# Values as the stationary operand in column tiles, and a gate that is turned instead of the heads, in the banded attention stage of a three-block kernel

## The reference, cut to what matters

```python
def swa_with_sinks(q, k, v, sinks):        # W = 128 queries a block, 256 keys for each
    ...
    s = jnp.where(mask[None, :, None, None], s, -jnp.inf)
    m = jnp.maximum(jnp.max(s, axis=-1, keepdims=True), sink)
    p = jnp.exp(s - m)
    denom = jnp.sum(p, axis=-1, keepdims=True) + jnp.exp(sink - m)
    p = (p / denom).astype(v.dtype)
    o = jnp.einsum('bnhgqk,bnkhd->bnqhgd', p, vw)
    return o.reshape(B, T, Hq * D)

# in first_block
o_a = swa_with_sinks(q_a, k_a, v_a, sinks[layer]) * jax.nn.silu(ag)
mix = jnp.concatenate([o_h, o_a], axis=-1)
out = jnp.einsum('bte,ed->btd', mix, w_out[layer])
```

## Time and profile before

| what | value |
|---|---|
| median of 3 runs | 4453.24 us (4452.0 to 4453.49) |
| the profiled execution, its own time | 4439.21 us |
| its span, first to last instruction | 4437.4 us |
| TensorE busy | 4089.6 us (92%), 26938 instructions |
| TensorE weight load busy | 3431.6 us (77%) |
| VectorE busy | 2470.0 us (56%) |
| ScalarE busy | 1464.4 us (33%) |
| GpSimd busy | 503.9 us (11%) |
| mean granted TensorE clock | 0.968 of 2.4 GHz |
| stage of the change in the trace | about 545 us to 1170 us of the span |

### The profile page before, as it was taken

How to read it: one execution, slowest core, us unless ns; L and a number is a source line. 1 busy time by engine, 2 the same in 40 slices (tenths; PEclk the granted TensorE clock), 3 DMA queues, 4 the chain that set the end, 5 groups by cost and what they waited for, 6 DMA issues and landing times. The chain is left out here.

```text
span 4437.4 us, 71865 instructions
## 1 busy us (share of the span) xinstructions
PE 4089.6 (92%) x26938; PEld 3431.6 (77%) x26938; DVE 2470.0 (56%) x5058; ACT 1464.4 (33%) x3233; POOL 503.9 (11%) x509
## 2 busy tenths in 40 slices
PE   9999889999699996999989978999898998999989
PEld 7888678888577775999878867778786776777767
DVE  5444444444467665777643347778643443677733
ACT  4232322222222222455521126666522221322221
POOL 0000011111100000122211100000000101122200
PEclk9999999999899998999989989999999999999989
DMA  4111321111434333121322244100045223323233
GB/s 151 50 66 50 109 94 64 64 64 64 150 126 145 121 127 102 50 69 57 123 97 111 112 141 144 39 20 29 17 169 183 102 104 138 127 90 102 90 136 118
DMA packets 218618, 434.72 MB, mean 98 GB/s; under 512 B 36803, under 2 KB 90692, under 8 KB 218278
## 3 DMA queue, kind: packets, MB, share of 16 engines
q1 hardware_dynamic: 218406, 431.89, 28.4%
HBM read 248.20 MB, written 146.93 MB: 89 GB/s over the span
## 5 line engine op out<-in xcount | busy, mean ns | idle before, releaser
L265 PE MATMUL rp_pj<-rp_w_high,rp_hT_high 128*128 128x512 f32 (+1 forms) x640 | 236.6, 379 | 23.2 <-DVE rp_gate L1443 17.8
L2652 DVE TENSOR_SCALAR_CACHE_REDUCE fa_sm<-fa_sc 128x512 f32<-128x512 f32 (+2 forms) x320 | 194.6, 610 | 92.7 <-PE fa_sc L2493 81.8
L265 PE MATMUL fp_pj<-fp_w_high,fp_hT_high 128*128 128x512 f32 (+2 forms) x640 | 216.6, 353 | 23.4 <-DMA fp_hT_low<-kept_low_dram 20.0
L266 PE MATMUL rp_pj<-rp_w_low,rp_hT_high 128*128 128x512 f32 (+1 forms) x640 | 231.7, 371 | 0.0
L266 PE MATMUL fp_pj<-fp_ahead_w_low,fp_hT_high 128*128 128x512 f32 (+2 forms) x640 | 214.7, 350 | 0.0
L265 PE MATMUL hg_pj<-hg_w_high,hg_hT_high 128*128 128x512 f32 x512 | 208.3, 407 | 5.2 <-DVE hg_w_low L255 5.2
L2600 ACT CAST fa_pT_high<-fa_tp 128x512 fp32r<-128x512 f32 (+1 forms) x288 | 160.9, 559 | 149.6 <-PE fa_tp L2507 147.5
L2507 PE MATMUL fa_tp<-fa_ident,fa_sm 128*128 128x128 f32 x1088 | 176.1, 283 | 31.9 <-DVE fa_pT_low L201 15.6
L265 PE MATMUL rc_pj<-rc_w_high,rc_hT_high 128*128 128x512 f32 (+1 forms) x512 | 190.6, 380 | 15.0 <-DMA rc_ident<-const_ident 10.0
L266 PE MATMUL hg_pj<-hg_w_low,hg_hT_high 128*128 128x512 f32 x512 | 201.5, 394 | 0.0
L2507 PEld LDWEIGHTS fa_tp<-fa_ident,fa_sm 128*128 128x128 f32 x1088 | 125.1, 142 | 93.4 <-DVE fa_pT_low L201 40.9
(11 more groups left out here) (590 smaller groups left out, 10843.8 us busy)
## 6 DMA issues: line engine op xcount, KB each, us to landing
rw_given<-rw_packed_dram SPq DMA_DIRECT2D x48, 512.0 KB, 3.7
rc_back<-rc_XB SPq DMA_DIRECT2D x48, 336.0 KB
rw_packed_dram<-rp_M SPq DMA_DIRECT2D x48, 256.0 KB, 2.6
rp_M<-rp_U SPq DMA_DIRECT2D x16, 728.0 KB, 4.7
hg_xt<-in_x SPq DMA_DIRECT2D x16, 512.0 KB, 3.6
kept_x_high_dram<-hg_hT_high SPq DMA_DIRECT2D x16, 512.0 KB, 3.5
kept_x_low_dram<-hg_hT_low SPq DMA_DIRECT2D x16, 512.0 KB, 4.3
sw_hT_high<-kept_x_high_dram SPq DMA_DIRECT2D x16, 512.0 KB, 3.6
```

The costliest lines, as they stand in the source:

```text
L265: pe.matmul(out, hT.high[:, kc, :], high[:, kc, lo:hi], start=kc == 0, stop=False)
L266: pe.matmul(out, hT.high[:, kc, :], low[:, kc, lo:hi], start=False, stop=False)
L2652: dve.tensor_scalar(sm[:, to:to + cols], bank_of(slot)[:, 0:cols], 0.0, NEG, ALU.add, ALU.max, accum_out=tops[:, four, c:c + 1]).then_inc( ...
```

## The change

The stationary and the moving operand of `weigh` change places. The values (128 keys x 64 numbers) become stationary, and the turned probabilities of two heads (128 keys x 256 columns) move. The 64 output numbers go to partitions 0 to 63 for even heads and to 64 to 127 for odd ones, so two neighbouring matmuls lie in different column tiles of the array. There are 8 matmuls instead of 16, and `ov` comes out with the head's numbers on its partitions and the queries in its columns.

So the result needs no turning, but the gate does, and the reciprocal sums, which are one number for each query and head, have to be multiplied into something that still has the queries on its partitions. VectorE multiplies the gate by `rden` into `gated` (between the reciprocal and its first copy of probabilities). TensorE turns `gated` into the bank `th` (`turn_gate`, between `turn_p` of rounds 2 and 3 and block 1 of `project_out`). ScalarE copies it to `gatedT` (between its copies of probabilities and the tanh). After `weigh`, one VectorE instruction makes `mixaT` from `ov` and `gatedT`, ScalarE rounds `mixaT` to `mixT.high`, and `low_of_mix` subtracts that from `mixaT`, both in SBUF. `turn_a` and the two instructions on `mixa` are gone. The semaphores follow; `turn_qk` now waits for the copies of the tile before, and `turn_hg` for `gatedT_ready`, since `th` is used twice in a tile.

```diff
--- before.py
+++ after.py
@@ -703,7 +703,9 @@
         sm = sb("sm", [P, SW_HEADS, 2 * P])
         top, negtop, sinkd, expsink, total, rden = (sb(n, [P, SW_HEADS]) for n in ("top", "negtop", "sinkd", "expsink", "total", "rden"))
         pT = sb("pT", [P, 2 * SW_HEADS, P])
-        mixa = sb("mixa", [P, SW])
+        gated = sb("gated", [P, SW])
+        gatedT = sb("gatedT", [P, 4, P])
+        mixaT = sb("mixaT", [P, 4, P])
         mixT = Parts(s, "mixT", [P, KC, P], STATIONARY)
         z = sb("z", [P, D])
         stats = sb("stats", [P, 2, 6])
@@ -725,7 +727,8 @@
         roped, v_kept, qk_turned, qT_ready, kT_ready = sem("roped"), sem("v_kept"), sem("qk_turned"), sem("qT_ready"), sem("kT_ready")
         scored, masked, top_ready, p_ready, den_ready = sem("scored"), sem("masked"), sem("top_ready"), sem("p_ready"), sem("den_ready")
         p_turned, pT_act, pT_dve, weighed, mixa_ready = sem("p_turned"), sem("pT_act"), sem("pT_dve"), sem("weighed"), sem("mixa_ready")
-        hg_turned, hgT_ready, a_turned, aT_ready = sem("hg_turned"), sem("hgT_ready"), sem("a_turned"), sem("aT_ready")
+        gated_ready, gate_turned, gatedT_ready = sem("gated_ready"), sem("gate_turned"), sem("gatedT_ready")
+        hg_turned, hgT_ready, aT_ready = sem("hg_turned"), sem("hgT_ready"), sem("aT_ready")
         out_done, z_ready, var_ready, rstd_ready, y_ready = sem("out_done"), sem("z_ready"), sem("var_ready"), sem("rstd_ready"), sem("y_ready")
         y_scaled = sem("y_scaled")
 
@@ -800,14 +803,15 @@
 
             def turn_qk(t, pt):
                 pe.wait_ge(roped, t + 1)
-                need(pe, aT_ready, t)
+                need(pe, pT_dve, 2 * t)
+                need(pe, pT_act, 2 * t)
                 for j in range(4):
                     pe.transpose(tp[0][:, j * P:(j + 1) * P], qkv[:, j * P:(j + 1) * P], ident[:])
                 pe.transpose(tp[1][:, 0:P], qkv[:, SW:SW + SW_KV], ident[:]).then_inc(qk_turned, 1)
 
             def turn_hg(t):
                 pe.wait_ge(hg_here, 16 * (t + 1))
-                need(pe, hgT_ready, t)
+                need(pe, gatedT_ready, t)
                 for c in range(4):
                     last = pe.transpose(th[:, c * P:(c + 1) * P], hgm[:, c * P:(c + 1) * P], ident[:])
                 last.then_inc(hg_turned, 1)
@@ -853,24 +857,26 @@
                         last = pe.transpose(tp[n % 2][:, m * P:(m + 1) * P], sm[:, k // 2, (k % 2) * P:(k % 2 + 1) * P], ident[:])
                     last.then_inc(p_turned, 1)
 
+            def turn_gate(t):
+                pe.wait_ge(gated_ready, t + 1)
+                pe.wait_ge(hgT_ready, t + 1)
+                for c in range(4):
+                    last = pe.transpose(th[:, c * P:(c + 1) * P], gated[:, c * P:(c + 1) * P], ident[:])
+                last.then_inc(gate_turned, 1)
+
             def weigh(t):
                 pe.wait_ge(pT_act, 2 * t + 2)
                 pe.wait_ge(pT_dve, 2 * t + 2)
                 pe.wait_ge(v_kept, t + 1)
                 need(pe, mixa_ready, t)
-                for j in range(4):
-                    for g in range(2):
-                        h = 4 * g + j
-                        for slot in range(2):
-                            last = pe.matmul(ov[:, h * SW_DIM:(h + 1) * SW_DIM], pT[:, 2 * (2 * j + g) + slot, :],
-                                             vr[:, slot, g * SW_DIM:(g + 1) * SW_DIM], start=slot == 0, stop=slot == 1)
+                for g in range(2):
+                    for slot in range(2):
+                        for odd in range(2):
+                            rows = slice(odd * SW_DIM, (odd + 1) * SW_DIM)
+                            first = 4 * odd + 2 * g + slot
+                            last = pe.matmul(heads(ov[rows, 2 * g * P:(2 * g + 2) * P], 2), vr[:, slot, g * SW_DIM:(g + 1) * SW_DIM],
+                                             pT[:, first:first + 9:8, :], start=slot == 0, stop=slot == 1)
                 last.then_inc(weighed, 1)
-
-            def turn_a(t):
-                pe.wait_ge(mixa_ready, t + 1)
-                for c in range(4):
-                    last = pe.transpose(tp[1][:, c * P:(c + 1) * P], mixa[:, c * P:(c + 1) * P], ident[:])
-                last.then_inc(a_turned, 1)
 
             def step(i, hi, pi, t, ht, pt):
                 p, m = i is not None, t is not None
@@ -896,10 +902,10 @@
                     turn_p(t, (0, 1))
                     project_out(t, 1, (0,))
                     turn_p(t, (2, 3))
+                    turn_gate(t)
                     project_out(t, 1, (1,))
                     weigh(t)
                     project_out(t, 1, (2, 3))
-                    turn_a(t)
                     project_out(t, 0, range(4, 8))
                     project_out(t, 1, range(4, 8))
 
@@ -933,6 +939,9 @@
                     for n in (0, 2):
                         act.wait_ge(p_turned, 4 * t + n + 1)
                         act.copy(pT[:, 4 * n:4 * n + 4, :], heads(tp[0][:], 4)).then_inc(pT_act, 1)
+                    act.wait_ge(gate_turned, t + 1)
+                    need(act, mixa_ready, t)
+                    act.copy(gatedT[:], heads(th[:], 4)).then_inc(gatedT_ready, 1)
                 if p:
                     if not m:
                         for c in range(2):
@@ -941,8 +950,8 @@
                     need(act, taken[2], i)
                     act.activation(tanh[:], pj[0][:], ACT.Tanh, scale=0.5).then_inc(tanh_ready, 1)
                 if m:
-                    act.wait_ge(a_turned, t + 1)
-                    act.copy(mixT.high[:, 4:8, :], heads(tp[1][:], 4)).then_inc(a_high, 1)
+                    act.wait_ge(mixa_ready, t + 1)
+                    act.copy(mixT.high[:, 4:8, :], mixaT[:]).then_inc(a_high, 1)
 
             pipeline(act, step)
 
@@ -988,7 +997,7 @@
 
             def low_of_mix(t, n):
                 dve.wait_ge((hg_high, a_high)[n], t + 1)
-                mixT.take_low(dve, lambda ap: ap[:, 4 * n:4 * n + 4, :], heads((th, tp[1])[n][:], 4)).then_inc((hgT_ready, aT_ready)[n], 1)
+                mixT.take_low(dve, lambda ap: ap[:, 4 * n:4 * n + 4, :], heads(th[:], 4) if n == 0 else mixaT[:]).then_inc((hgT_ready, aT_ready)[n], 1)
 
             def softmax(t, pt):
                 by_group = sm[:].rearrange("p (j g) k -> p j g k", g=2)
@@ -1013,6 +1022,11 @@
                 dve.tensor_tensor(total[:], total[:], expsink[:], ALU.add)
                 dve.drain()
                 dve.reciprocal(rden[:], total[:])
+                dve.drain()
+                by_group = rden[:].rearrange("p (j g) -> p g j", g=2).unsqueeze(3).to_broadcast([P, 2, 4, SW_DIM])
+                need(dve, gate_turned, t)
+                dve.tensor_tensor(gated[:].rearrange("p (g j d) -> p g j d", g=2, j=4), gate2[:].rearrange("p (g j d) -> p g j d", g=2, j=4),
+                                  by_group, ALU.mult).then_inc(gated_ready, 1)
                 for n in (1, 3):
                     dve.wait_ge(p_turned, 4 * t + n + 1)
                     dve.tensor_copy(pT[:, 4 * n:4 * n + 4, :], heads(tp[1][:], 4)).then_inc(pT_dve, 1)
@@ -1035,11 +1049,9 @@
                     softmax(t, pt)
                     dve.drain()
                     dve.wait_ge(weighed, t + 1)
-                    by_group = rden[:].rearrange("p (j g) -> p g j", g=2).unsqueeze(3).to_broadcast([P, 2, 4, SW_DIM])
-                    dve.tensor_tensor(mixa[:].rearrange("p (g j d) -> p g j d", g=2, j=4), ov[:].rearrange("p (g j d) -> p g j d", g=2, j=4),
-                                      by_group, ALU.mult)
-                    dve.drain()
-                    dve.scalar_tensor_tensor(mixa[:], mixa[:], 0.5, gate2[:], ALU.mult, ALU.mult).then_inc(mixa_ready, 1)
+                    dve.wait_ge(gatedT_ready, t + 1)
+                    need(dve, a_high, t)
+                    dve.scalar_tensor_tensor(mixaT[:], heads(ov[:], 4), 0.5, gatedT[:], ALU.mult, ALU.mult).then_inc(mixa_ready, 1)
                 if p:
                     dve.drain()
                     dve.wait_ge(tanh_ready, i + 1)
```

## The result

The changed kernel takes 4402.09 us (median of 4 runs, 4401.14 to 4403.47) against 4452.62 us, a ratio of 0.9888 with an interval of 0.987 to 0.9905. It is 50.5 us faster. I had said 4412.2 with a range of 4403 to 4426, so the sign and the cause were right, and the time is 10.1 us under the forecast and 0.9 us under the range. Its profiled execution takes 4402.16 us, span 4400.3, no different from its median.

The account below looks back on a forecast made before the run. TensorE was taken to bound the stage; 15 steady tiles at 2.53 us plus 3.0 for the last gave 41.0 us, so 4398.2 profiled and, with the median 14.0 higher, 4412.2 us (chance 0.75), range 4403 to 4426.

Parts of the forecast that it names:

- The bound: Stage of the change: TensorE sets the pace, busy 35.24 of 36.88 us a step, at full clock.
- the price of `weigh`: New `weigh` on TensorE: 16 records of 256 columns run in pairs, 1.87 us, ends 1.7 and 5.7.
- B: Rival: `weigh`'s pairs run in series, 1.73 us more a tile, total 4439.7 us; chance 0.06.
- D: Rival: each change of column tile empties the array and reloads, `weigh` 5.7 us, total 4473.5; chance 0.03.
- A: Rival: column-tile weight loads in `weigh` aren't hidden, 0.4 us a tile, total 4418.6 us; chance 0.08.
- The stretch: From the end of `turn_p` to block 4 of `project_out`: 8.43 us before, a steady tile gains 2.53.
- the copy of keys and values before `low`: VectorE's queue before block 4: copy from 822.85 to 823.27, `low_of_mix` right behind it, 0.69 us.
- The cover before `weigh`: `turn_gate` moves `weigh` to after 819.3, so VectorE's second copy of probabilities, done at 819.06, costs no stop.
- The last tile: No next gate or keys, so `low` waits for ScalarE; block 4 at 823.48, a gain of 3.0 us.
- Rival C: `low_of_mix` with two SBUF inputs loses the port to GpSimd: 1.3 us in 15 steps, total 4431.7; chance 0.05.
- the median of the runs stands 14.0 higher, and a difference carries over: Whole program: median 4453.24 against profiled 4439.21, so 4398.2 for a like profiled execution becomes 4412.2 us.
- 4 us either way for stretches at half clock: Program's 284 us at the 1.2 GHz level may change once everything behind starts 41 us earlier; 1.4% of them.

Follow-up runs that it names:

- the three padded kernels: Idle two-column matmuls added behind the last `project_out`: 16 to the kernel before, 4443.00 us; 64 to it, 4452.44; 48 to the changed kernel, 4410.24.
- the halved kernels: Changed kernel with `weigh` and the steps behind it cut in two by key head: 4384.80 us; with 16 two-column matmuls added, 4388.48.

## Why the prediction was right about the change and wrong about the time

**The bound, and the price of `weigh`: right.** 1.87 us by `score` and the pooling, measured 1.88. The run without column tiles shows that it is the pairs that shorten it, so B and D fall. A falls too: with loads laid bare, `weigh` would have been 2.3. The Trainium skill ("TensorE: Matmul & The Clock Gate", Part 3, The mechanism) has the rule behind A, that weight loads overlap matmuls only where the row groups differ; the 1.88 us here speak against it for column tiles.

**The stretch: right, 0.07 short.** A steady tile gained 2.60 us (8.47 to 5.87, from the last transpose of `turn_p` to block 4) where I had 2.53. TensorE's wait is 1.00 to the row and 1.17 from start to start (807.44 + 0.23 = 807.67 to 808.84), where I had 1.25. The term that was mis-sized is the copy of keys and values before `low`: I let it run to its end, 0.42, and the next instruction starts 0.34 after it. The cover before `weigh` held. The last tile gained 3.0, as said. In the stage that is 42.1 us against 41.0. Two of my additions are slightly off: 823.27 + 0.69 + 0.05 is 824.01, not 823.99, which takes 0.3 us off the 41.0, and B's gain is 13.3 us, not 13.5.

**Rival C: right to give it little.** `low_of_mix` with two SBUF inputs takes 0.68, and GpSimd's first instruction takes 0.66 where it took 0.35: it is the one that waits. Where `low` doesn't stand beside it, in the kernel with VectorE's order changed, it takes 0.35 again. It ends at 808.99, 0.2 after `low`, so this row agrees with the Trainium skill ("SBUF — State Buffer", Who interferes with whom): the one issued first keeps the port.

**The failed step: "the median of the runs stands 14.0 higher, and a difference carries over".** It took the distance between one profiled execution and the median as a constant of measuring. In the changed kernel that distance is 0.1 us (4402.16 against 4402.09). In the kernel before it was another stage, rw, which is 12 us longer where the clock falls before its work is over; the runs have that, to judge by their times, and the profiled one happened not to have it. The change moved the instruction blocks of all that follows by 192 instructions, the stop in the rw stage went, and the distance went with it: 50.5 is 41 for the change and 9 for the place of the blocks. I had allowed 4 us either way for stretches at half clock. That term should have had the 14 us that I had before my eyes, as a gain if it vanished, and the range would have reached 4398 at least. That the time came to lie as near as 0.9 us to the range is luck: 14.0 us too much were carried over, and some 4 us in other stages went against it. My sum for a profiled execution like the first was 4398.2, and it took 4402.16, with fp, fa and po 4.9 us longer than in the first, a difference between executions that I can't explain. And the row was in the trace from which I predicted: TensorE waiting on "issue" for 1.0 us in line 1659, the longest such wait in the middle of a line, in a stage that I didn't read because the change doesn't touch it.

What isn't shown: that a late instruction block is what TensorE waits for. The packet that ends 1.2 to 1.5 us before TensorE goes on, the lack of a semaphore, and the three padded kernels speak for it; the halved kernels, whose runs are long and short with the padding and without, don't settle it. Nor is it shown why the clock held in the one execution that had the stop.

## What to carry to other kernels

In a kernel like this, where a head is 64 wide, try the values stationary in column tiles and the gate turned instead of the result: here two tiles streamed at once, and the turning left the path behind the softmax. When that is done, look at what still stands behind the last matmul; here, in halves, it hid under blocks that don't need it. When an edit changes how many instructions an unrolled program has, be ready for a shift from stages that it doesn't touch (here 8 to 9 us, 0.2%). Compare with some dummy instructions added (here 64) before you credit it to the edit. And where a profiled execution stands off the median of its kernel by more than the runs' own spread, find out in which stage before you carry the difference over.

## What the runs showed of the hardware that I had not expected

TensorE stopped for 0.7 to 1.3 us between two matmuls of the rw stage without any semaphore, and each time it went on 1.2 to 1.5 us after the end of an instruction packet. In the kernel before, 64 instructions more in an idle place, 1 us of work, took the stop away, and 256 brought it back. With the stop, the granted clock fell to the 1.2 GHz level while 18 to 24 us of dense work were left, in five of the six profiled executions with the stop; that made the stage some 10 to 12 us longer. The pairing of column tiles worked over matmuls that aren't neighbours in the program (1.93 us against 1.88).
